# Attention beside an expert stream: the causal mask moved to TensorE, sums of squares per head to ScalarE, and the last products of a stage issued two by two

## The reference

```python
# stick_breaking, 16 heads of 64, for each query block
z = einsum(q, k) * scale
valid = key_pos < q_pos
log_keep = where(valid, log_sigmoid(-z), 0)
after = reversed cumulative sum of log_keep, minus log_keep
wgt = where(valid, exp(log_sigmoid(z) + after), 0)      # times v
# q and k: rmsnorm over each head's 64 columns first
# peer, per token: 8 heads, 2 x 128 sub-keys, top 16 of each half -> top 16 experts
out = sum_k softmax(best)_k * gelu(u[expert_k] . h) * v[expert_k]
```

## Time and profile before

| | |
|---|---|
| runs, median (lowest to highest) | 2005.23 us (2003.51 to 2007.88) |
| the profiled execution | 2004.27 us, span 2002.5 us |
| mean granted TensorE clock | 0.817 |
| busy: PE, DVE, ACT, POOL | 1477.6, 1187.2, 279.0, 1025.1 us |
| read from memory | 667.68 MB, 334 GB/s over the span |

### The profile page before, as it was taken

The page is one execution under the profiler, slowest core; times in us unless marked ns, Lnnn a source line. Parts: engine busy times, 40 slices in busy tenths (PEclk is TensorE's granted clock), DMA queues, the critical chain, the costliest instruction groups (busy, mean ns, idle before and its releaser), DMA issues.

```text
span 2002.5 us, 19164 instructions
## 1 busy us (share of the span) xinstructions
PE 1477.6 (74%) x6422; PEld 588.6 (29%) x6422; DVE 1187.2 (59%) x2799; ACT 279.0 (14%) x539; POOL 1025.1 (51%) x1099
## 2 busy tenths in 40 slices
PE   6979999784667556668888885687797866656666
PEld 5736666474233110102223222022232210101100
DVE  3641000258787756787669636976786587777752
ACT  2141111211001100001212111012321110010000
POOL 2000000004777766676556655774565677677675
PEclk9988999887688866768996998689988976677668
DMA  9113346106999999999999999999989999999998
GB/s 330 62 75 137 132 162 266 59 22 216 381 409 409 409 409 410 406 409 384 409 403 346 410 409 387 410 408 409 397 325 409 410 410 409 399 410 409 397 400 328
DMA packets 189387, 669.93 MB, mean 335 GB/s; under 512 B 19806, under 2 KB 20960, under 8 KB 188016
## 3 DMA queue, kind: packets, MB, share of 16 engines
q0 software_dynamic: 152064, 553.72, 70.4%
q1 hardware_dynamic: 37232, 115.09, 15.1%
HBM read 667.68 MB, written 1.05 MB: 334 GB/s over the span
## 4 chain that ended last, share of the span: by engine, by line
DMA 30%; POOL 14%; PE 14%; DVE 13%; issue 7%; DVEq 2%; ACT 1%; POOLq 0%; ACTq 0%
DMA big<-in_peer_v,expert 21%; POOL big L505 14%; DMA big<-in_peer_u,expert 9%; DVE big L568 8%; PE ps L551 4%; PE ps L691 3%; PE ps L534 2%; PE ps L334 2%; DVEq L446 2%; PE ps L785 1%; DVE residual L598 0%; PE ps L787 0%; PE ps L1657 0%; DVE half_v L452 0%; DVE diag L585 0%
## 5 line engine op out<-in xcount | busy, mean ns | idle before, releaser
L551 PE MATMUL ps<-big,diag 128*32 128x512 f32 (+1 forms) x2112 | 710.4, 792 | 438.8 <-DMA big<-in_peer_v,expert 403.1
L568 DVE CUSTOM_DVE_ANT_0 big<-big,ps 128x1024 f32<-128x1024 f32 x528 | 625.4, 1218 | 332.4 <-DMA big<-in_peer_u,expert 229.4
L505 POOL DMA_INDIRECT big<-in_peer_u,expert x528 | 501.6, 950 | 319.2 <-issue 133.8
L505 POOL DMA_INDIRECT big<-in_peer_v,expert x528 | 506.8, 960 | 249.3 <-PE ps L551 132.5
L551 PEld LDWEIGHTS ps<-big,diag 128*32 128x32 f32 (+1 forms) x2112 | 83.5, 121 | 972.3 <-DMA big<-in_peer_v,expert 848.0
L691 PE MATMUL ps<-big 128*128 128x512 f32 x384 | 195.4, 632 | 1.0 <-ACT big L880 1.0
L1585 POOL MEMSET big<- 128x128 f32 x3 | 0.5, 202 | 373.9 <-POOLq L1449 373.9
L230 DVE RECIPROCAL stats<-stats 128x1 f32<-128x1 f32 (+1 forms) x17 | 2.8, 162 | 252.0 <-ACT stats L224 251.5
L1505 PE MATMUL ps<-ua,big 128*128 128x256 f32 x512 | 116.3, 382 | 0.0
L1516 PE MATMUL ps<-big,sc 128*128 128x512 f32 x256 | 114.4, 592 | 0.0
L1505 PEld LDWEIGHTS ps<-ua,big 128*128 128x128 f32 x512 | 98.3, 192 | 25.4 <-issue 13.2
(11 more groups left out here) (293 smaller groups left out, 1201.6 us busy)
## 6 DMA issues: line engine op xcount, KB each, us to landing
big<-in_mlp_w SPq DMA_DIRECT2D x16, 2048.0 KB, 7.8
big<-in_w_kv SPq DMA_DIRECT2D x32, 512.0 KB, 6.9
big<-in_peer_wq SPq DMA_DIRECT2D x32, 512.0 KB, 6.8
big<-in_w_in SPq DMA_DIRECT2D x5, 2048.0 KB, 17.6
big<-in_peer_u,expert POOLq DMA_INDIRECT x528, 10.3
big<-in_peer_v,expert POOLq DMA_INDIRECT x528, 10.3
big<-in_peer_wq SPq DMA_DIRECT2D x1, 8192.0 KB, 27.2
big<-in_w_q SPq DMA_DIRECT2D x16, 512.0 KB, 6.9
```

The source lines that it names most:

```text
L505: nc.gpsimd.indirect_dma_start(out=ring[n % len(ring)], out_offset=None, in_=rows[name], in_offset=bass.IndirectOffsetOnAxis(ap=expert[:, ...
L551: last = nc.tensor.matmul(acc[r:r + tokens, :], placed(u, tokens)[:, k, :], ring_v[n % len(ring_v)][:, BANK * half:BANK * (half + 1)], sta ...
L568: nc.vector.tensor_tensor_reduce(out=slot, in0=slot, in1=rows_x, scale=1.0, scalar=0.0, op0=ALU.mult, op1=ALU.add, accum_out=dots[:, u % 2 ...
```

## The change

Three edits, all in the attention pieces.

1. **Mask.** `hidden` holds -1e30 above and on the diagonal and 0 elsewhere. `scores_z` adds it with one more product per head, identity times `hidden`, into the last 128 columns of z. The sigmoid of z is then 0 there and "keep" is 1. VectorE's last product (L1061) and the drain before it are gone, and the running product takes `nothing`, a plane of zeros, in place of `unseen`. GpSimd makes the planes in 3 instructions instead of 4.
2. **Sums of squares.** ScalarE squares each head's 64 columns in an instruction of its own with an accumulated sum, 16 per result (and 8 for the meta tokens' k), and takes the root in the same piece; `a_raw` comes after the root. VectorE's reductions, `a_sums` and `a_roots` are gone, and VectorE waits for `a_raw` one step later, where it scales.
3. **Two by two.** In the last step of each product stage (the one that holds chunk 7) the chunks are issued in pairs: chunks 4 and 5 at q = 0, 6 and 7 at q = 1, or 6 and 7 at q = 0 in a stage of 3+3+2. Before, there was one chunk per q.

```diff
+        def part(ks, q):
+            return ks[2 * q:2 * q + 2] if len(ks) and ks[-1] == KD - 1 else ks[q:q + 1]
...
-            for k in share(t, AT_Q, i, "q")[q:q + 1]:
+            for k in part(share(t, AT_Q, i, "q"), q):
                 product(pe, t, C_Q, k, q_in[:, k, :], 4)
...
             def scores_z(n):
                 if n == 0:
+                    pe.wait_ge(S("masks_ready"), 3)
...
-                    last = m.matmul(bank(4 + e)[:, 0:z_at], q_t[r:r + HD, n, :], k_t[r:r + HD, n, 0:z_at],
-                                    start=True, stop=True)
+                    m.matmul(bank(4 + e)[:, 0:z_at], q_t[r:r + HD, n, :], k_t[r:r + HD, n, 0:z_at], start=True, stop=False)
+                    last = m.matmul(bank(4 + e)[:, z_at - P:z_at], ident[:], hidden, start=False, stop=True)
...
+            def head_roots(product, rows, at):
+                heads = 16 if at == 0 else 8
+                for head in range(heads):
+                    a.activation(sq[0:rows, HD * head:HD * (head + 1)], product[:, HD * head:HD * (head + 1)], ACT.Square,
+                                 accum_out=head_sums[0:rows, at + head:at + head + 1])
+                act.drain()
+                last = a.activation(head_sums[0:rows, at:at + heads], head_sums[0:rows, at:at + heads], ACT.Sqrt,
+                                    scale=1.0 / HD, bias=eps_col[0:rows])
+                if at == 0:
+                    last.then_inc(S("a_raw"), 1)
...
-                a.activation(sq, bank(4, 2), ACT.Square).then_inc(S("a_raw"), 1)
+                head_roots(bank(4, 2), P, 0)
...
-            for n, at in enumerate((AT_Q + 1, AT_K + 2 - t)):
+            for n, at in enumerate((AT_Q + 2, AT_K + 3 - t)):
                 if i == at:
                     dve.wait_ge(S("a_raw"), ONE["a_raw"] * t + n + 1)
-                    v.tensor_reduce(head_sums[:, 0:16], sq.rearrange("p (h c) -> p h c", c=HD), X, ALU.add)\
-                        .then_inc(S("a_sums"), 1)
...
-                                             unseen[:, L - z_at:L][:, ::-1], 1.0, ALU.mult, ALU.max)
+                                             nothing[:, 0:z_at], 1.0, ALU.mult, ALU.max)
                     dve.drain()
-                    v.tensor_tensor(s, s, kp[:, :, 1:z_at + 1], ALU.mult)
-                    dve.drain()
-                    v.tensor_tensor(s[:, :, z_at - P:], s[:, :, z_at - P:], seen.unsqueeze(1).broadcast_to([P, 2, P]),
-                                    ALU.mult).then_inc(S("a_w"), 1)
+                    v.tensor_tensor(s, s, kp[:, :, 1:z_at + 1], ALU.mult).then_inc(S("a_w"), 1)
```

More of the change, by code:

```diff
@@ L178, in program @@
         wq_peer = cut(big, W, KD, 2 * D)
-        unseen, seen = big[:, 15488:15488 + L], big[:, 15776:15776 + P]
+        nothing, hidden = big[:, 15488:15488 + L], big[:, 15776:15776 + P]
         ring_w = [big[:, W + D * i:W + D * (i + 1)] for i in range(RING_W)]
@@ L726, in attend_pe @@
                 pe.wait_ge(S("a_raw"), 1)
-            for k in share(t, AT_K, i, "k")[q:q + 1]:
+            for k in part(share(t, AT_K, i, "k"), q):
                 product(pe, t, C_K, k, x_in[:, k, :], 6, 4 if t == 0 else None)
@@ L741, in attend_pe @@
                 pe.wait_ge(S("a_raw"), ONE["a_raw"] * t + 2)
-            for k in share(t, AT_V[t], i, "v")[q:q + 1]:
+            for k in part(share(t, AT_V[t], i, "v"), q):
                 product(pe, t, C_V, k, x_in[:, k, :], 6, 4 if t == 0 else None)
@@ L797, in attend_pe @@
                     pv(n - 4)
-            for k in {5: range(0, 4), 6: range(4, 8)}.get(loop, ())[q:q + 1]:
+            for k in part({5: range(0, 4), 6: range(4, 8)}.get(loop, range(0)), q):
                 if k == 0:
@@ L814, in attend_pe @@
                     {11: (1, range(0, 3)), 12: (1, range(3, 6)), 13: (1, range(6, 8))}.get(loop, (1, ())):
-                for k in ks[q:q + 1]:
+                for k in part(ks, q):
                     product(pe, t, C_P + KD * half, k, hnt[:, k, at:at + P], 6 - 2 * half)
@@ L885, in attend_act @@
                     a.activation(raw_m, bank(4)[0:HD], ACT.Copy)
-                    a.activation(kn_m, bank(4)[0:HD], ACT.Square)
                 a.activation(raw, bank(6, 2), ACT.Copy)
[L888 to L896, removed]
+                if t == 0:
+                    head_roots(bank(4)[0:HD], HD, 16)
+                head_roots(bank(6, 2), P, 0)
             if AT_KT[t] <= i < AT_KT[t] + 3 - t:
@@ L1015, in attend_dve @@
                          "a_inputs")
-            for n, at in enumerate((AT_Q + 1, AT_K + 2 - t)):
+            for n, at in enumerate((AT_Q + 2, AT_K + 3 - t)):
                 if i == at:
                     dve.wait_ge(S("a_raw"), ONE["a_raw"] * t + n + 1)
-                    if n == 1 and t == 0:
-                        v.tensor_reduce(head_sums[0:HD, 16:24], kn_m.rearrange("p (h c) -> p h c", c=HD), X, ALU.add)
-                    v.tensor_reduce(head_sums[:, 0:16], sq.rearrange("p (h c) -> p h c", c=HD), X, ALU.add)\
-                        .then_inc(S("a_sums"), 1)
-            for n, at in enumerate((AT_Q + 2, AT_K + 3 - t)):
-                if i == at:
-                    dve.wait_ge(S("a_roots"), ONE["a_roots"] * t + n + 1)
                     if n == 1:
@@ L1048, in attend_dve @@
                     v.memset(keep[t][:, :, z_at:z_at + 1], 1.0)
-                    dve.wait_ge(S("masks_ready"), 4)
+                    dve.wait_ge(S("masks_ready"), 3)
                     dve.drain()
@@ L1588, in _ @@
                 g = nc.gpsimd
-                step(pool, g.memset(unseen, 0.0), "masks_ready")
-                step(pool, g.affine_select(out=unseen[:, L - P:], in_=unseen[:, L - P:], compare_op=ALU.is_gt, fill=1.0,
-                                           base=0, pattern=[[-1, P]], channel_multiplier=1), "masks_ready")
-                step(pool, g.memset(seen, 1.0), "masks_ready")
-                step(pool, g.affine_select(out=seen, in_=seen, compare_op=ALU.is_gt, fill=0.0,
-                                           base=0, pattern=[[-1, P]], channel_multiplier=1), "masks_ready")
+                step(pool, g.memset(nothing, 0.0), "masks_ready")
+                step(pool, g.memset(hidden, 0.0), "masks_ready")
+                step(pool, g.affine_select(out=hidden, in_=hidden, compare_op=ALU.is_gt, fill=NEG, base=0,
+                                           pattern=[[-1, P]], channel_multiplier=1), "masks_ready")
                 peer_gpsimd(pool)
```

## The result

| | before | after |
|---|---|---|
| runs, median (lowest to highest) | 2006.29 us (2001.56 to 2011.97), 22 runs | 2016.42 us (2004.64 to 2022.03), 22 runs |
| ratio after / before | | 1.0046, interval 1.0036 to 1.0057 |
| the profiled execution | 2004.27 us, span 2002.5 | 2018.25 us, span 2016.1 |
| mean granted TensorE clock | 0.817 | 0.812 |
| busy: PE, DVE, ACT, POOL | 1477.6, 1187.2, 279.0, 1025.1 us | 1497.7, 1177.0, 288.3, 1022.6 us |

A forecast was written before the change was run, and what follows sets the result against it. The prediction took the DMA's gather stream as the bound, with TensorE late in the score loops, which lose 20 us. Tile 0 -5.0, tile 1 +1.5, rest 0: -3.5 on 2004.3, so 2000.8, or 2001.7 for the median; range 1995 to 2009.5.

The forecast's parts named there:

- Part 1, the price of a mask: Score loops: two mask products per head pair cost TensorE 0.48 us at full clock, 0.87 at half; VectorE saves 0.49.
- the block of the earlier trace: 32 TensorE records of 128 columns by 128-column weights, 3.81 us at full clock, from which the mask was priced.
- The 0.87 "from above": Upper limit taken for a pair's two mask products at half clock, from slot values: 1.92 us at half, 1.05 at full.
- Tile 0: First tile's score loop: an earlier mask shortens TensorE's 2.86 us wait, the clock stays full, 5.0 us won.
- The forecast of 5.2 us per period: First tile's loop at full clock, z to z: 3.4 us work, 1.3 waiting for ACT, 0.48 mask; the DMA needs 5.12.
- The 5.0 us of gain: First tile's two loop stretches: of 5.8 us lost some 1.4 stay; of 2.5, 0.6 goes.
- Tile 1: Second tile's score loop: the clock falls as before, masks cost 2.7 us less 1.2 of wait, 1.5 us lost.
- Part 2: ScalarE's sums of squares: 0.45 us per head, 7.2 for 16; TensorE's waits covered by the DMA queue, cost 0.
- Part 3: Product stages, chunks issued two by two: worth 0 by itself, within 1 us either way.
- half clock in both loops, the mask paid by PE: Rival for both tiles' score loops: +1.1 and +1.5 us, together +2.6, 2007.8 us; chance 0.22.
- full clock in both loops: Rival for both tiles' score loops: -5 us in the first, -3.5 in the second, 1996.7 us; chance 0.22.
- the two signs that were to show the forecast wrong: First tile's projection stretch under 400 GB/s, or GpSimd waiting in the loops for DVE rather than PE.

The follow-up runs named there:

- after_again: The kernel after, word for word, measured and profiled once more on a faster chip: ratio 1.0054 to the kernel before.
- roots_only: The kernel before with only the sums of squares and roots moved to ScalarE, on a faster chip: ratio 0.9990.
- pairs_only: The kernel before with only the last product chunks issued two by two, on a faster chip: ratio 1.0001.
- split_bf16: The kernel after with both heads' z first, then both masks, as bfloat16 products, on a faster chip: ratio 0.9949 to the kernel before.
- before_again: The kernel before, word for word, run as a candidate against itself on a faster chip: ratio 1.0006.
- between_bf16: The kernel after with the mask products in bfloat16, still between the two heads' z, on a faster chip: ratio 1.0026 to the kernel before.

## Why the prediction was wrong, step by step

**Part 1, the price of a mask: this step failed.** The step said "PE gains two products of 128 columns by 128-column weights, 4 records", priced at 0.48 us at full clock and 0.87 at half. It failed twice. The smaller part is the products themselves: start to next start they take 0.75 and 1.32 us, since the block of the earlier trace rows, 0.12 us per record, isn't what a record costs here (0.21 and 0.17). The greater part is that I added only records. The place of the added product took away an overlap that the kernel before had, worth 0.65 and 1.20 us per pair. A hint stood in the earlier trace rows: at the block's 0.12 us per record of 128 columns, four records of 144 columns take 0.54 us at full clock and 1.07 at half (an estimate), and the group took 0.85 at half, as long as two of its records take now. It was no more than a hint, for at the rate of slot values the same estimate is 0.54 at half. The 0.87 "from above" was no bound, since it bounded the product and not what it separates. The experiments put the weight on this second part: with the masks in bfloat16 the order alone is worth 0.77%.

**Tile 0.** DVE's saving came as worked out: behind the weight (L1062, start 1443.66) the next scan starts 0.64 us later, for 0.65 forecast. The first wait of TensorE for the weights was 3.84 us and is 1.03; the one of 2.86 us is gone. Behind the first wait the clock was at half for some 3 us, as before; then it stayed at full through what had been the second wait, as forecast, and through a first wait of 0.95 us for a sigmoid, but fell behind the second:

```profile
1052.65 0.38 PE L775 MATMUL ps<-ident,big 128*16 128x128 f32 x1 [1.03 <-DVE big L1062]
...
1066.54 0.48 PE L765 MATMUL ps<-ua 64*128 64x144 f32 x2
...
1068.13 0.27 PE L775 MATMUL ps<-ident,big 128*16 128x128 f32 x1
...
1069.69 0.65 PE L790 MATMUL ps<-big,normed 128*64 128x128 f32 x2 [0.95 <-ACT big L939]
...
1073.98 0.85 PE L765 MATMUL ps<-ua 64*128 64x144 f32 x2
...
1076.84 0.42 PE L775 MATMUL ps<-ident,big 128*16 128x128 f32 x1
```

A pair's z and masks take 1.59 us at full clock (1066.54 to 1068.13) for about 0.44 before, and 2.86 at half for 0.78. The forecast of 5.2 us per period counted 0.48 for this. The first two periods at full clock were 4.45 us (1056.40 to 1060.85) and 5.69 (to 1066.54), about what the DMA needs, so the stretch up to 1075 rose from 375 to 379 GB/s; behind the fall it lost more than it had won: 298 for 330. The 5.0 us of gain came out as 2.1 us of loss. In after_again the clock held until about 1073 us, its periods at full clock were 5.05, 5.70 and 5.66 us, and 3.2 of the 5.0 us were won. So in tile 0 the forecast had the way right in one trace and not in the other; what fell short in both is the price of the mask.

**Tile 1.** The wait of 2.66 us for a sigmoid stayed and the clock fell behind it, both as forecast. 1.5 us of loss were forecast; by the stretches it was 13.4. The forecast had 2.7 us for the last four masks; at the measured price they are 1.39 + 3 x 2.5 = 8.9, 6.2 more. That leaves 13.4 - 1.5 - 6.2 = 5.7 us, which go with a half clock that lasted 41 us instead of 16 (how long it lasts without a mask between varies, 6 to 25 us). The prediction let the clock fall as before; that it would stay down longer was in no term.

**Part 2.** ScalarE's squares were priced too high. After's timeline of ScalarE:

```profile
1353.78 0.34 ACT L876 ACTIVATE big<-ps 128x64 f32<-128x64 f32 x1
1353.89 0.32 ACT L876 ACTIVATION_READ_ACCUMULATOR big<-ps 128x1 f32 x1
1353.98 0.34 ACT L876 ACTIVATE big<-ps 128x64 f32<-128x64 f32 x1
```

One head starts 0.20 us behind the other (1353.78 to 1353.98), since an instruction and its read (0.34 and 0.32 us) overlap with those that follow. 16 heads took 3.1 us, where 7.2 were forecast and 6.4 was to be the least. So TensorE didn't wait 5 us ahead of tile 0's k product: in the whole trace it waits for ScalarE's root once, 1.45 us ahead of tile 0's v product. That the DMA covers it was right, and roots_only shows it at 0.9990.

```profile
999.95 3.78 PE L695 MATMUL ps<-big 128*128 128x512 f32 x4 [1.45 <-ACT head_sums L879]
```

As before, a slot value behind it waits longer than that for its rows: 3.43 us, at 1035.48.

**Part 3,** worth 0, holds (pairs_only 1.0001).

**The rivals.** The one on the other side of zero, "half clock in both loops, the mask paid by PE", had the mechanism: TensorE the last engine, the mask on its path at half clock. Its price, 0.87, was the failed one, so it ended at 2007.8, and the measured time lay beyond the range. For "full clock in both loops" stood that there would be more full-width products; in tile 1 they came, and the clock stayed at half for longer in both traces of the kernel. Neither of the two signs that were to show the forecast wrong came: the projections ran at 409 GB/s, and GpSimd waited in tile 1's loop for PE (17.3 us) rather than for DVE (2.6). Both signs tested who is late, and neither the price of the mask.

## What to carry to other kernels

An instruction put between two others costs more than its own duration if they overlapped. Before adding one, compare the time of the group in which it goes with the sum of its members; if the group is shorter, put the new one ahead of it or behind it. The members' times have to come from rows of the same shape alone; from other shapes the sum is only an estimate. And an engine whose clock has two levels may pay it again: here 1.2 us more per pass of the loop went with a pass that was 3.9 us longer.

## What the runs showed of the hardware

- Two score products with weights of 64 rows, in the lower and the upper half of the partitions, take 0.66 us together when adjacent and 0.65 us each with a product of 128 rows between them (272 columns, float32, full clock). The Trainium skill ("TensorE: Matmul & The Clock Gate", Part 3) says that products in different row groups of the array run at the same time; the trace agrees: at half clock both heads together take 1.28 us, and one alone 1.27.
- Between two score products a 128 x 128 mask product takes 0.42 us at full clock and 0.73 at half in float32 (L766, start to next start), against 0.24 for two records in the block of the earlier trace rows; in bfloat16 the record of it lasts 0.23 and 0.29 us (L768), and that of two behind each other 0.29 and 0.39.
- The time at half clock isn't set by the idling ahead of it alone: behind the same 2.66 us it lasted 7 us in split_bf16, 16 in before, 7 in before_again, the same kernel, and 25 in pairs_only, but 41 in after, 41 in its second trace and 44 in between_bf16. TensorE was busy 37.02 of the 40 us from 1460 to 1500 in after, at a granted clock of 0.63. By the Trainium skill's rule that sustained activity releases the throttle (same page, Part 1) this stretch would show 1.00; the trace disagrees. What about a mask between the heads keeps it there is open, and with it whether the longer half clock is a cause of its own or follows from the longer period.
- On chips where the stream runs slower, parts 2 and 3 together cost 0.36 and 0.50% in two comparisons; on a faster chip neither of them cost anything by itself (0.9990 and 1.0001). Which of them, and by what wait, stays open.
